# Last two attention units of a fused decoder trunk: order of scores and output products, share of the norms, buffers of the third output piece

## What is computed

```python
def sliding_window_attention(h, w_qkv, q_gain, k_gain, sinks):
    qkv = jnp.einsum('bld,de->ble', h, w_qkv)
    ...
    q = rms_norm(q, q_gain) * (HEAD_DIM ** -0.5)
    k = rms_norm(k, k_gain)
    ...
    s = jnp.einsum('bnqhgd,bnkhd->bhgnqk', qb, kw)
    ...
    s = s - slopes * dist.astype(f32)
    s = jnp.where(valid, s, -jnp.inf)
    ...
    m = jnp.maximum(jnp.max(s, axis=-1, keepdims=True), sink)
    p = jnp.exp(s - m)
    p = p / (jnp.sum(p, axis=-1, keepdims=True) + jnp.exp(sink - m))
    o = jnp.einsum('bhgnqk,bnkhd->bnqhgd', p, vw)
    return o.reshape(bsz, seqlen, Q_WIDTH)
...
            mix = jnp.einsum('blc,cd->bld', att, odd_out_proj[j])
        x = x + mix.astype(x.dtype)
        h = rms_norm(x, moe_norm[layer])
        ffn = hierarchical_moe(h, ...)
        x = x + ffn.astype(x.dtype)
```

## Time and profile before

| | us |
|---|---|
| median of 3 runs | 862.59 |
| lowest, highest | 862.09, 864.71 |
| the profiled execution: whole time | 864.32 |
| the profiled execution: span of its instructions | 862.60 |

### The profile page before, as it was taken

The page is one execution under the profiler, slowest core; times in us unless marked ns, Lnnn a source line. Parts: engine busy times, 40 slices in busy tenths (PEclk is TensorE's granted clock), DMA queues, the critical chain, the costliest instruction groups (busy, mean ns, idle before and its releaser), DMA issues.

```text
span 862.6 us, 11120 instructions
## 1 busy us (share of the span) xinstructions
PE 793.6 (92%) x4248; PEld 555.6 (64%) x4248; DVE 597.6 (69%) x815; ACT 468.6 (54%) x639; POOL 170.5 (20%) x169
## 2 busy tenths in 40 slices
PE   5999999999999899998998999999789899999992
PEld 4454555555688777777875554657468777777771
DVE  4699964866554788887886356666344788888880
ACT  4032302823334387787884027776734488787781
POOL 5400001500001233332310001042101223323311
PEclk9999999999999899999999999999899999999997
DMA  9321120203452499999977000132062599999952
GB/s 371 133 95 49 51 80 19 98 1 145 200 215 100 177 417 340 326 320 324 311 274 289 25 0 1 49 147 98 0 268 98 203 408 341 325 314 335 325 159 31
DMA packets 31451, 160.94 MB, mean 187 GB/s; under 512 B 7601, under 2 KB 7729, under 8 KB 16032
## 3 DMA queue, kind: packets, MB, share of 16 engines
q1 hardware_dynamic: 18432, 130.03, 39.6%
q0 software_dynamic: 11232, 24.60, 10.0%
q10 hardware_dynamic: 1728, 5.52, 1.7%
HBM read 152.32 MB, written 24.12 MB: 205 GB/s over the span
## 4 chain that ended last, share of the span: by engine, by line
PE 51%; DVE 16%; DMA 14%; ACT 8%; issue 4%; POOL 2%; DVEq 2%; POOLq 2%; ACTq 0%
DMA ring<-stream 14%; PE PS L1927 9%; PE PS L1740 8%; PE PS L2056 8%; PE PS L2167 8%; DVE w_lo L958 6%; PE PS L2080 3%; DVE arena L958 3%; ACT w_hi L654 2%; PE PS L2202 2%; PE PS L1872 2%; PE PS L2215 2%; PE PS L2225 1%; PE PS L1957 1%; DVE left_hi L958 1%
## 5 line engine op out<-in xcount | busy, mean ns | idle before, releaser
L958 DVE TENSOR_TENSOR w_lo<-ring,w_hi 128x2048 fp32r<-128x2048 f32 x92 | 209.7, 2288 | 46.1 <-ACT w_hi L654 39.6
L654 ACT ACTIVATE w_hi<-ring 128x2048 fp32r<-128x2048 f32 x86 | 164.4, 1915 | 38.6 <-DMA ring<-stream 34.0
L2056 PE MATMUL PS<-w_hi,left_hi 128*128 128x512 f32 x512 | 175.7, 405 | 9.5 <-DVE left_hi L958 9.2
L2056 PEld LDWEIGHTS PS<-w_hi,left_hi 128*128 128x128 f32 x512 | 96.9, 189 | 32.3 <-DVE left_hi L958 13.3
L2056 PE MATMUL PS<-w_lo,left_hi 128*128 128x512 f32 x256 | 100.7, 393 | 0.0
L2080 PE MATMUL PS<-w_hi,left_lo 128*128 128x512 f32 x256 | 84.8, 392 | 4.4 <-DVE left_lo L958 2.4
L2167 PE MATMUL PS<-ring,hT 128*128 128x512 f32 (+1 forms) x192 | 74.9, 537 | 0.9 <-DVE hT L958 0.9
L512 POOL DMA_INDIRECT arena<-rows x32 | 47.8, 1495 | 64.4 <-PE PS L2033 50.9
L2080 PEld LDWEIGHTS PS<-w_hi,left_lo 128*128 128x128 f32 x256 | 48.0, 188 | 16.8 <-issue 4.2
L1740 PE MATMUL PS<-ring,hT 128*128 128x512 f32 x128 | 57.6, 600 | 0.4 <-ACT arena L710 0.4
L1740 PE MATMUL PS<-hT,ring 128*128 128x512 f32 x128 | 56.4, 596 | 0.8 <-ACT arena L710 0.8
(11 more groups left out here) (275 smaller groups left out, 1362.2 us busy)
## 6 DMA issues: line engine op xcount, KB each, us to landing
ring<-stream SPq DMA_DIRECT2D x110, 1024.0 KB, 17.1
arena<-stream SPq DMA_DIRECT2D x6, 1024.0 KB
rows<-arena POOLq DMA_DIRECT2D x8, 512.0 KB, 3.0
x<-stream SPq DMA_DIRECT2D x4, 1024.0 KB
x<-x_in SPq DMA_DIRECT2D x4, 512.0 KB, 5.5
x<-x_in ACTq DMA_DIRECT2D x4, 512.0 KB, 4.2
sums<-x POOLq DMA_DIRECT2D x4, 512.0 KB, 3.8
x<-sums SPq DMA_DIRECT2D x4, 512.0 KB, 5.1
```

The source lines that it names most:

```text
L654: act.activation(w_hi[pair], held_slot(layer, m), ACT.Copy).then_inc(w_hi_done, 1)
L958: return V.tensor_tensor(out, a, b, op)
L2056: ins = mm(PS[:, 2, :], a, b, start=k == 0 and t == 0, stop=k == KD - 1 and t == 2)
```

## The change

Four things, all in layer 1 but for index tables that give layer 0 what it had:

- PE: from unit 6 on, products are cut into halves (`front`, `back`: six matmuls each) and the scores stand between them. Unit 7's scores come earlier: `att_scores(7, 0)` goes from behind `out_second(1)` and the second half of unit 5's turns to between that unit's two turns, and `att_scores(7, 1)` behind the first half of `out_second(1)`. Unit 7's first turns go ahead of unit 6's attend.
- DVE: `biased(7, 0)` goes ahead of `most(6)`, and `most(7)` ahead of `summed(6)`. So the semaphore `m_done` counts otherwise in the last units (`most_done`, `sum_inverted`). The odd heads of units 6 and 7 are normed by DVE (four tensor_scalar each). Three of the four adds of the first half go up among the last units. ACT: `exps(7)` follows `exps(6)` with one copy between them, the odd norms of units 6 and 7 are gone.
- Piece 2 gets pair 1, piece 3 pair 0. `weights_hi(1, 2)` waits for the last scores and turned queries and stands ahead of `attended_hi(7)`, its low part behind `attended(7)`; `weights_hi(1, 3)` now waits for the last use of piece 0.
- `kn` and `v_rows` swap places in the arena; the experts of layer 1 take their buffer pairs in the same order as layer 0.

```diff
+        def out_pair(layer, s):
+            return ((1, 0, 1, 0), (0, 2, 1, 0))[layer][s]
         def out_hi(layer, s):
-    return w_lo2[:, :] if layer and s == 1 else w_hi[(s + 1 - layer) % 2]
+    return w_lo2[:, :] if layer and s == 1 else w_hi[out_pair(layer, s)]
...
+def most_done(u):
+    return 14 if u == 7 else 2 * u + 1
+def sum_inverted(u):
+    return 15 if u == 6 else 2 * u + 2
...
             def weights_hi(layer, s):
...
-                if s == 2:
+                if s == 2 and layer:
+                    act.wait_ge(s_psum, 16)
+                    act.wait_ge(qtr_psum, 3 * TT)
+                if s == 2 + layer:
                     act.wait_ge(w_used, used(layer, -1))
-                if s == 3:
-                    act.wait_ge(mix_psum, 8 * layer + TT)
+                if s == 3 and layer == 0:
+                    act.wait_ge(mix_psum, TT)
...
+            def normed_odd(u):
+                pr = probs[u % 2]
+                dve.drain()
+                for h in range(1, 8, 2):
+                    ins = ts(pr[:, h, :], pr[:, h, :], asum[u % 2][:, h:h + 1], ALU.mult)
+                ins.then_inc(p_norm_odd, 1)
...
             heads_and_values(3)
-            out_second(0)
+            front, back = (0, 1), (2, 3)
+            out_second(0, front)
             att_scores(6, 1)
+            out_second(0, back)
             turn_probs(5, 0)
-            out_second(1)
+            att_scores(7, 0)
             turn_probs(5, 1)
-            att_scores(7, 0)
-            out_first(2)
+            out_second(1, front)
             att_scores(7, 1)
             attend(5, 0)
             attend(5, 1)
+            out_second(1, back)
+            out_first(2)
             turn_probs(6, 0)
+            out_second(2, front)
             turn_probs(6, 1)
-            out_second(2)
+            out_second(2, back)
+            turn_probs(7, 0)
             attend(6, 0)
             attend(6, 1)
-            turn_probs(7, 0)
             turn_probs(7, 1)
-            out_first(3, (0, 1))
+            out_first(3, front)
             attend(7, 0)
             attend(7, 1)
-            out_first(3, (2, 3))
+            out_first(3, back)
             out_second(3)
```

More of the change, by code:

```diff
@@ L938, in _ @@
                 turned_probs(a, 0)
-                if more:
-                    head_deviation(n + 1)
+                head_deviation(n + 1)
                 turned_probs(a, 1)
                 exps(b)
+            attended_hi(4)
+            normed_odd(5)
+            turned_probs(5, 0)
+            turned_probs(5, 1)
+            exps(6)
+            attended_hi(5)
+            exps(7)
+            turned_probs(6, 0)
+            turned_probs(6, 1)
+            turned_probs(7, 0)
             attended_hi(6)
-            normed_odd(7)
-            turned_probs(7, 0)
             turned_probs(7, 1)
+            weights_hi(1, 2)
             attended_hi(7)
@@ L1314, in token_rows @@
                     stt(row_tile[tt], x[:, tt, :], rstd[:, tt:tt + 1], gain_row, ALU.mult, ALU.mult).then_inc(rows_made, 1)
[L1316 to L1320, removed]
-                    tt_(xv, xv, mixed(layer, half, tt), ALU.add).then_inc(mix_done, 1)
-                weights_lo(layer, 2)
-                for tt in range(TT):
-                    add(0, tt)
+                if layer == 0:
+                    weights_lo(0, 2)
+                for tt in range(3 * layer, TT):
+                    add(layer, 0, tt)
                 weights_lo(layer, 3)
@@ L1638, in _ @@
                 most(a)
-                if more:
-                    raw(n + 1, 1)
+                raw(n + 1, 1)
                 biased(b, 0)
@@ L1643, in _ @@
                 biased(b, 1)
-                if more:
-                    raw(n + 1, 2)
-                    head_sums(n + 1)
+                raw(n + 1, 2)
+                head_sums(n + 1)
                 if n:
                     attended(a - 1)
-                if more:
-                    normed_heads(n + 1)
+                normed_heads(n + 1)
                 most(b)
+            heads_out(3)
+            biased(6, 0)
+            summed(5)
+            attended(4)
+            biased(6, 1)
+            biased(7, 0)
+            most(6)
+            biased(7, 1)
+            most(7)
+            summed(6)
+            normed_odd(6)
+            attended(5)
+            summed(7)
+            normed_odd(7)
+            add(1, 0, 0)
+            add(1, 0, 1)
             attended(6)
-            summed(7)
+            add(1, 0, 2)
             attended(7)
+            weights_lo(1, 2)
             residual(1)
```

62 lines of the change are left out of this document (31 added, 31 removed).

## The result

The changed kernel takes **858.12 us** (median of 8 runs, 856.02 to 861.46). The kernel before, run beside it, takes 865.24 (8 runs, 861.7 to 867.88). The ratio is **0.993**, with an interval of 0.9903 to 0.9957: faster by 0.4 to 1.0%. It compares the runs and isn't the quotient of the two medians, which would be 0.992; of 865.24 us it makes 6.1 us (3.7 to 8.4). The eight runs of before include the three known at the time of the prediction (862.59, 864.71, 862.09). The five new ones are 861.7, 865.77, 866.09, 866.21 and 867.88, so the median from which I subtracted lay 2.65 us too low. The forecast's saving was 7.3 us; the two medians differ by 7.1.

The account below looks back on a forecast made before the run. PE was taken to bound the stretch before 655 us, through holes of 4.82 and 3.42 us and low clock behind them. Terms 1.7 + 0.5 + 3.4 + 1.5 + 0.2 = 7.3 gave 855.3 us, range 852.9 to 858.2.

Parts of the forecast that it names:

- 1.7 earlier: On PE, `out_first(3)` would start at 623.1 instead of 624.80: 1.7 us of the saving.
- I take the clock as low for 3 us after the hole: On PE from 613.5 on: low clock assumed for 3 us, as after the old hole of 3.42 us.
- hole before unit 6's turns: PE would idle 2.7 us there, waiting for POOL's norm at 612.3; the old 4.82 hole moved and made smaller.
- odd norm of unit 6 on DVE: Four tensor_scalar on DVE, blocked 1.9 us by POOL's norm, then 1.3: 3.2 us, one instruction near 2.2.
- idle before piece 2: PE would not wait before piece 2's first product, its low part on DVE hidden with 0.8 us to spare.
- loads of 684.46: The next weight loads, after the first gather, would start near 677.2 instead of 684.46.
- The terms 0.5, 3.4, 1.5 and 0.2: PE savings: `out_first(3)` off low clock 0.5; piece 2's idle 3.4 and low clock 1.5; small gaps 0.2 us.
- The behind part: Sign of failure: time from first token turn to the end, 208 us, changing by more than 1.
- gain absorbed: Rival: the DMA-bound expert stage's start hangs on something that doesn't move, nothing saved, 862.6 us; chance 0.07.
- Shorter hole: Rival: clock does not fall, 854.5, or DVE is not blocked either, 853.6 us; chance 0.20.
- Longer low clock: Rival: PE at half rate from 613 to 621 us, losing 4 instead of 1: 858.2; chance 0.20 with "Late on DVE".
- Late on DVE: Rival: unseen DVE wait between 600.6 and 609.9 lengthens the hole 1 to 3 us; chance 0.20 with "Longer low clock".

Follow-up runs that it names:

- e1: The changed kernel run once more with no edit; 857.31 us, ratio 0.9889 to the kernel before.
- e10: The changed kernel run a third time with no edit; 856.67 us (one run).
- e2: The changed kernel with 22 transposes without use in PE's hole before unit 6's turns; 855.74 us, ratio 0.9884 to the kernel before.
- e3: The changed kernel with VectorE's maximum of unit 6 moved ahead of `biased(7, 0)`; 853.58 us, ratio 0.9848 to the kernel before.
- e7: The changed kernel with both halves of the norms of units 6 and 7 on VectorE, none on POOL; 859.34 us, ratio 0.9928 to the kernel before.
- e12: The changed kernel with unit 6's maximum earlier, all norms of units 6 and 7 on VectorE, three `out_second(2)` products behind unit 6's attend; 853.87 us, ratio 0.9855.
- e4: The kernel before with only the buffer part and its waits, piece 2's high part ahead of `attended_hi(7)`; 860.72 us, ratio 0.9942.
- e5: The changed kernel with piece 2 back in pair 0, piece 3 in pair 1, old waits, high part behind `attended_hi(7)`; 860.62 us, ratio 0.9926.
- e6: The changed kernel with the odd heads' norms of units 6 and 7 back on ScalarE; 861.32 us, ratio 0.9949 to the kernel before.

## Why the prediction came out as it did

The direction and the mechanism were right, and the saving nearly: forecast 7.3 us, 7.1 between the medians, 6.1 by the ratio, 6.6 in the stretch by the mean of the profiles. The number itself, 855.3, is 2.8 us too low. Two steps failed: the base of the subtraction, which makes 2.65 of the 2.8, and one term of the sum, which was mis-sized. That the medians come so near to 7.3 is in part luck, since they also hold what varied outside the stretch. Of the stretch the forecast makes 65.74 − 7.3 = 58.4; the three profiles have 59.74, 58.41 and 58.74.

**The point from which I subtracted.** I took 862.59, the median of three runs, and found it well matched by the span, 862.6. Eight runs gave 865.24, and three later sets of before on other occasions 865.2, 865.95 and 866.31. I had said how the span stands to the median, and not how far a median of three may be from that of many: 2.65 us here. Subtracting from the profiled execution's whole time, 864.32, would have given 857.0, but nothing then on record said that this one execution was the better base.

**The term "1.7 earlier" of the sum, the mis-sized one.** `out_first(3)` starts 35.64 us behind the stretch's start (622.20 − 586.56) instead of 35.94 (624.80 − 588.86): 0.3 earlier in the first profile of after. The hole ended 0.3 later than forecast (612.60 in before's time, where I had 612.3). The other 1.1 is the step "I take the clock as low for 3 us after the hole": it was low for about 6.1 us of the stage of 6.20. In e1 it was 3.1, and there the start is at 34.31, 1.6 earlier, nearly as forecast; in e10 it is at 34.64, 1.3 earlier. The rows that I had showed all these lengths: about 3 us behind the second hole and 4.9 behind the first, which is the nearer in kind (turns behind a wait for POOL), and most of 8 in the earlier trace rows. I took the shortest as the value and made the longest a rival; it is rather one term with a spread, 0.8 to 2.15 us by e2, of which the forecast took the good side.

Point by point, with 2.30 us added to times of after to bring them to before's:

| step of the prediction | forecast | measured |
|---|---|---|
| `most(6)`, start | 602.3 | 602.5 |
| `exps(6)`, start | 605.4 | 605.6 |
| `most(7)`, start | 606.9 | 607.2 |
| hole before unit 6's turns | 2.7 | 2.79 (2.79, 2.77 in the repeats) |
| odd norm of unit 6 on DVE; its first instruction | 3.2; near 2.2 | 2.81; 2.03 |
| low clock behind the hole | 3 | 6.1 (3.1; in e10 3.4, from 0.5 behind PE's return on) |
| idle before `out_first(3)` | 0.6 | 0.49 |
| `out_first(3)`, start | 623.1 | 624.5 |
| from `out_first(3)` to the first token turn, shorter by | 5.6 | 29.80 − 24.10 = 5.7 |
| idle before piece 2 | 0 | 0 |
| first token turn | 647.3 | 648.6 |
| loads of 684.46 | 677.2 | 676.68 + 2.30 = 679.0 |
| first token turn to the end, change | under 1 | 1.2 (0.7, 0.2) |

`most(7)` is the chain's first line above (604.91), `most(6)` the line at 600.24 under e3, and `exps(6)` this one of ACT:

```profile
603.29 0.51 ACT L901 ACTIVATE arena<-arena,small 128x256 f32<-128x256 f32 x1 [4.16 <-DVE small L978]
```

*Norm on DVE.* That DVE waits for POOL was the reading of one row at 32 us; it held: the first of the four instructions takes 2.03 us of the 2.81, where the others take 0.34 each, and unit 7's first one takes 2.03 as well. By the rule of the Trainium skill, page "SBUF — State Buffer", section "Who interferes with whom", that a VectorE instruction in a two-port mode and a GpSimd instruction on SBUF exclude one another, and that the one that issues second is blocked for the whole of the first, the trace agrees. e7 shows the other half of it: without GpSimd's instruction each of VectorE's takes 0.35 us, though the drain ahead of them is still there. The forecast's 3.2 was 0.4 too long: three further instructions took 0.78, and the first ended 0.15 us behind POOL's (610.40 against 610.25), where I had let all four, 1.3 us, follow POOL's end.

*Piece 2.* The low part was hidden at the place forecast, with 0.7 us to spare where I had 0.8: piece 2's first product starts at 629.98. On DVE and ACT of after:

```profile
626.99 2.28 DVE L975 TENSOR_TENSOR w_lo<-ring,w_hi 128x2048 fp32r<-128x2048 f32 x1
```

```profile
622.28 1.92 ACT L635 ACTIVATE w_hi<-ring 128x2048 fp32r<-128x2048 f32 x1
```

The high part runs from 622.28 and the low part ends at 629.27, without a gap on PE anywhere in 20.70 us. The terms 0.5, 3.4, 1.5 and 0.2 sum to 5.6 and measured 5.7.

*The behind part.* I had called the prediction wrong if the time behind the first token turn changed by more than 1 us. It changed by 1.2, but the repeats (208.7 and 208.2, and 208.6 for before) say that this is the spread of that part, which reaches from 207.4 to 212.5 over all fourteen profiles. The criterion was too tight; it needed a second profile of before.

*The loads.* Until the first token turn after is 6.0 us earlier, and the loads 5.5 (679.0 against 684.46): the saving moves the DMA stage as a whole, and "gain absorbed" falls, as e3 and e12 show again with the full gain in their times.

**Rivals.** "Shorter hole" (the clock doesn't fall) isn't what the changed kernel did, but it is what e3, e7 and e2 made of it. "Longer low clock" is what the first profile comes nearest to: low for 6.1 us behind the hole where the rival had 8, and a stretch 1.3 us longer than forecast where it had 3; e1 and e10 are nearer to the forecast. That the median, 858.12, is so near to this rival's 858.2 is chance, as 2.65 us of its distance from 855.3 are the base. "Late on DVE" falls: the hole was 0.1 longer than forecast.

**Two sums of the prediction are off by 0.1.** The hole of unit 6, from 609.7 to 612.3, is 2.6 us and not 2.7, and the longer low clock, 3 us more than 855.3, comes to 858.3 and not 858.2. Neither changes a reading.

**What each part brings**, in us of the stretch: the free pair 3.7 alone and 1.7 on top of the rest (e4, e5); VectorE's half of the norms 3.0 (e6); the new order, on balance, nothing measurable without VectorE's half (e6 against e4), and no run has VectorE's half without the new order. As it was written the new order also costs some 1.7 of idle time and 0.8 to 2.15 of low clock that one exchange on DVE gives back (e3). What stays open is why the clock fell at different moments of the same hole (0.8 us ahead of its end in the first profile, 0.5 behind it in e10) and why it stayed low for 6.1 us behind it once and for 3.1 at another time, with the same work.

## What to carry to other kernels

Where an engine waits for another's result before step B, look whether an independent step A that stands behind B in its order fits into the wait: that exchange was worth 3 us of the stretch here. Before GpSimd and VectorE are given two halves of one step on SBUF at the same time, try VectorE alone: here it did all of it in 2.19 us, less than its half had taken (2.81), though the timed runs don't show the gain. And before a small gain is forecast, count how wide the base is: give the term for the clock behind a hole all of the lengths that the rows show, and don't rest a number to 0.3% on three runs.

## What the runs showed of the hardware that I had not expected

- Behind the same hole (2.79, 2.79 and 2.77 us of idle PE) the granted clock came back 6.1, 3.1 and 3.9 us after PE's return. It had fallen 0.8 and 0.2 us ahead of that return in the first two, and 0.5 us behind it in the third (e10), when PE was at work again. Behind holes of 2.03 (e7), 1.07 (e4) and 1.03 us (e3) it stayed at 1.00 in the profile.
- When a GpSimd instruction on SBUF starts 0.02 us ahead of VectorE's, VectorE's waits for it: 2.03 us for one that takes 0.35 alone, ended 0.15 us behind GpSimd's. Back to back such an instruction of 128x256 costs 0.26 us (eight in 2.19, the last one with its whole 0.35).
- With the code unchanged, the part ahead of the stretch varied from 586.2 to 591.2 us and the part behind it from 207.4 to 212.5. A difference of two spans of single profiles can be off by some 5 us for that alone; the length of the touched stretch repeated within 0.3 us for the kernel before.
